# A two-block transformer kernel: gates and inverse roots of the output stages by exponential and logarithm, with the window and attention stages in another form

## The reference

```python
p = softmax(q k^T * scale + c_q - c_k, causal);  oa = (p v) * silu(za)        # forgetting attention
p = softmax([q k^T * scale in the band, sink]);  ob = (p v) * silu(zb)        # window attention
y = concat(oa, ob) @ w_out;  x = x + gate * y * rsqrt(mean(y*y) + 1e-6) * g   # first output stage
...
h = layer_norm(2**0.25 * h + concat(a * silu(ga), r * silu(gh)) @ w_out_2)    # second output stage
```

## Time and profile before

| what | value |
|---|---|
| time, median of 3 runs | 4440.61 us (4437.15 to 4445.45) |
| time of the profiled execution | 4440.12 us |
| its span, first to last instruction | 4438.6 us |
| busy: PE, DVE, ACT, POOL | 80%, 49%, 32%, 22% of the span |
| mean granted TensorE clock | 0.873 |

### The profile page before, as it was taken

How to read it: one execution, slowest core, us unless ns; L and a number is a source line. 1 busy time by engine, 2 the same in 40 slices (tenths; PEclk the granted TensorE clock), 3 DMA queues, 4 the chain that set the end, 5 groups by cost and what they waited for, 6 DMA issues and landing times. The chain is left out here.

```text
span 4438.6 us, 48060 instructions
## 1 busy us (share of the span) xinstructions
PE 3551.6 (80%) x16984; PEld 2783.3 (63%) x16984; DVE 2178.9 (49%) x4079; ACT 1440.1 (32%) x2352; POOL 996.4 (22%) x1050
## 2 busy tenths in 40 slices
PE   8299999466669999796799997935554699999978
PEld 7299988355646665675577776834444266666657
DVE  0600000322256665442489999845564345455456
ACT  0200000112124444441258873233332223333344
POOL 0120111212133320101322322343433033123010
PEclk9599999677779999898899998967777689999989
DMA  4121121200032321535212353411100454544254
GB/s 142 60 92 58 60 74 66 73 10 9 12 77 61 75 67 35 170 129 184 71 44 74 95 160 89 137 64 38 38 19 25 134 147 116 122 104 118 79 174 140
DMA packets 347338, 382.06 MB, mean 86 GB/s; under 512 B 95092, under 2 KB 276404, under 8 KB 340196
## 3 DMA queue, kind: packets, MB, share of 16 engines
q1 hardware_dynamic: 243144, 272.58, 21.6%
q10 hardware_dynamic: 98368, 77.62, 5.9%
q0 software_dynamic: 5632, 29.36, 1.7%
HBM read 260.26 MB, written 119.20 MB: 85 GB/s over the span
## 5 line engine op out<-in xcount | busy, mean ns | idle before, releaser
L447 DVE COPY p_stage<-p_bank 128x512 f32<-128x512 f32 (+4 forms) x78 | 43.3, 555 | 643.7 <-PE p_bank L409 643.7
L2429 PE MATMUL cbank<-hT_high,cw_hi 128*128 128x512 f32 x800 | 321.6, 402 | 37.9 <-POOL kpartsI L2401 16.9
L2608 DVE TENSOR_SCALAR_CACHE_REDUCE sharedI<-xI,TI 128x384 bf16<-128x384 f32 (+8 forms) x284 | 348.9, 1294 | 0.1
L2126 DVE CUSTOM_DVE_ANT_0 n_junk<-n_pM,n_chosen 128x512 bf16<-128x512 f32 (+4 forms) x352 | 200.7, 571 | 300.5 <-PE n_pM L1997 176.8
L2429 PE MATMUL cbank<-hT_high,cw_lo 128*128 128x512 f32 x800 | 315.9, 395 | 0.0
L2081 ACT ACTIVATE n_PT<-n_pS 128x512 f32<-128x512 f32 (+4 forms) x352 | 177.4, 504 | 426.6 <-PE n_pS L2035 425.1
L2429 PE MATMUL cbank<-hT_low,cw_hi 128*128 128x512 f32 x800 | 315.6, 395 | 0.0
L2052 PE MATMUL n_pO<-n_PT,n_vv 128*128 128x512 f32 (+4 forms) x704 | 315.4, 530 | 0.0
L2544 ACT ACTIVATE sharedI<-xI,biasI 128x2048 bf16<-128x2048 f32 (+2 forms) x192 | 289.8, 1511 | 48.5 <-DVE biasI L2614 48.5
L2052 PE MATMUL f_pO<-f_PT,f_vv 128*128 128x512 f32 (+3 forms) x640 | 292.6, 539 | 0.0
L2121 DVE TENSOR_REDUCE f_mxc<-f_pM 128x1 f32<-128x512 f32 (+2 forms) x320 | 190.3, 598 | 148.8 <-PE f_pM L1990 78.8
(11 more groups left out here) (432 smaller groups left out, 8755.2 us busy)
## 6 DMA issues: line engine op xcount, KB each, us to landing
n_mkt<-scratch_mask_turned ACTq DMA_DIRECT2D x256, 128.0 KB, 2.1
cw_raw<-in_w_in_dram SPq DMA_DIRECT2D x50, 512.0 KB, 4.7
wa<-in_w_ada_dram SPq DMA_DIRECT2D x16, 768.0 KB, 4.3
n_rawk<-scratch_keys SPq DMA_DIRECT2D x16, 516.0 KB, 10.0
xt<-in_x_dram POOLq DMA_DIRECT2D x16, 512.0 KB, 3.8
scratch_qk<-p_stage ACTq DMA_DIRECT2D x32, 256.0 KB, 2.4
f_rawq<-scratch_qk SPq DMA_DIRECT2D x16, 512.0 KB, 7.8
f_rawk<-scratch_qk SPq DMA_DIRECT2D x16, 512.0 KB, 9.5
```

What stands on the lines that cost most here:

```text
L447: v.tensor_copy(stage[0:rows, k, 0:width], bank[0:rows, k, 0:width]).then_inc(s_evac[k], 1)
L2126: v.tensor_tensor_reduce(junk[:, n % 2, 0:wd], pM[:, n % 2, 0:wd], chosen[:, at:at + wd], 1.0, 3.0 * NEG, ALU.add, ALU.max, accum_out=to). ...
L2429: last = pe.matmul(bank[:, p % RING, 0:wd], lhsT=w_part[pw][b][:, c, :], rhs=rhs, start=(c == 0 and a == 0), stop=(c == DC - 1 and a == 2))
L2608: own_.up(v.tensor_scalar(junk_v[:, own_.at % 2, 0:(i + 1) * P], scores(i), T[:, j:j + 1], None, compare, ALU.add, accum_out=count[:, j:j ...
```

## The change

Beside the output stages, the diff gives the window stage and the attention stages another form.

- Output stages: the gate becomes exp, log, exp on ACT, each waiting for the one before. The root becomes log and exp on ACT. DVE's mean square and reciprocal go.
- Window stage: `KZ` goes; keys are copied by one instruction, and the score product contracts over the group's own 64 partitions.
- Attention stages: `times_gate` and the folding go. DVE weighs 64 partitions x 512 columns, inverts 2 x 256 columns, multiplies by the gate from SBUF, then by the output from PSUM, which frees the output's buffer only then. Maxima are rounded and split into two columns by three further small instructions, turned by a transpose. `lead` is one less. Blanking moves from DVE to GpSimd, ahead of its constants and splits; the splits are one instruction each; the `n_` stage waits for all masks and both bias parts at its start.

The core of the diff:

```diff
@@ stage_window
-                v.tensor_copy(KZ[0:HD, par, 0, :], pT[0:HD, 0, :])
-                v.tensor_copy(KZ[HD:P, par, 1, :], pT[HD:P, 0, :]).then_inc(s_T, 1)
+                v.tensor_copy(T[:, par, 4, :], pT[:, 0, :]).then_inc(s_T, 1)
+                half = slice(HD * g, HD * g + HD)
-                        last = pe.matmul(pS[:, g, j, z, :], lhsT=T[:, par, j, :], rhs=KZ[:, kp, g, :],
+                        last = pe.matmul(pS[:, g, j, z, :], lhsT=T[half, par, j, :], rhs=T[half, kp, 4, :],
@@ stage_out, ScalarE
-                act.activation(sig[:], zg[:, b, :], ACT.Sigmoid).then_inc(s_sig, 1)
+                own_.up(act.activation(sig[:], zg[:, b, :], ACT.Exp, scale=-1.0))
+                own_.settle()
+                own_.up(act.activation(sig[:], sig[:], ACT.Ln, bias=1.0))
+                own_.settle()
+                act.activation(sig[:], sig[:], ACT.Exp, scale=-1.0).then_inc(s_sig, 1)
-                act.wait_ge(s_var, n + 1)
-                act.activation(std[:, b:b + 1], var[:, b:b + 1], ACT.Sqrt).then_inc(s_std, 1)
+                own_.settle()
+                if n >= 2:
+                    act.wait_ge(s_res[b], r)
+                own_.up(act.activation(rstd[:, b:b + 1], ssq[:, b:b + 1], ACT.Ln, bias=eps[:, 0:1], scale=1.0 / D))
+                own_.settle()
+                act.activation(rstd[:, b:b + 1], rstd[:, b:b + 1], ACT.Exp, scale=-0.5).then_inc(s_root, 1)
@@ stage_out, VectorE
-                v.wait_ge(s_ssq, n + 1)
-                v.tensor_scalar(var[:, one], ssq[:, one], 1.0 / D, 1e-6, ALU.mult, ALU.add).then_inc(s_var, 1)
-                v.wait_ge(s_std, n + 1)
-                own_.up(v.reciprocal(rstd[:, one], std[:, one]))
-                own_.settle()
+                v.wait_ge(s_root, n + 1)
@@ stage_attend
-        self.lead = self.tiles(NJ - 1) + 5
+        self.lead = self.tiles(NJ - 1) + 4
-            return sw.block_ends_with_unit(u - 3 + LEAD)
+            return sw.block_ends_with_unit(u - 2 + LEAD)
@@ stage_attend, GpSimd (start, then each head)
+            for b in range(2):
+                step(gp.memset(QA[b][HD:P, :].bitcast(F32), 0.0))
+                step(gp.memset(KA[b][HD:P, :].bitcast(F32), 0.0))
+            for b in range(2):
+                if cum2 is not None:
+                    step(gp.memset(QA[b][HD:HD + 2, :].bitcast(F32), 1.0))
+                step(gp.memset(KA[b][96:98, :].bitcast(F32), 1.0))
+            step(gp.memset(vv[:, 0, :, HD:P], 1.0))
+            step(gp.memset(vv[:, 1, :, 0:HD], 1.0))
-                for at in pieces(S):
-                    last = gp.tensor_tensor(QL[b][lower, at], rawq[lower, at], QA[b][lower, at].bitcast(F32), ALU.subtract)
-                last.then_inc(s_split, 1)
+                gp.tensor_tensor(QL[b][lower], rawq[lower], QA[b][lower].bitcast(F32), ALU.subtract).then_inc(s_split, 1)
@@ stage_attend, TensorE (values)
-                        pe.wait_ge(s_oz, B - 1)
+                        pe.wait_ge(s_norm, B - 1)
@@ stage_attend, VectorE
+                    own_.up(v.tensor_reduce(mx[:, a:b], mxc[:, B % 2, a:b, 0:n], AX.X, ALU.max))
+                own_.settle()
+                own_.up(v.tensor_scalar(mh[:], mx[:], -1.0, None, ALU.mult))
+                own_.settle()
+                own_.up(v.tensor_copy(Mx[:, :, 96], mh[:].bitcast(F32)))
+                v.scalar_tensor_tensor(Mx[:, :, 97], mx[:], -1.0, mh[:].bitcast(F32), ALU.mult, ALU.subtract
+                                       ).then_inc(s_stat, 1)
-                    last = v.tensor_reduce(Mx[:, a:b, 96], mxc[:, B % 2, a:b, 0:n], AX.X, ALU.max)
+                v.scalar_tensor_tensor(w[out], ez[den, B % 2], 1.0, pO[den, B % 2], ALU.add, ALU.mult).then_inc(s_w, 1)
-                own_.up(v.reciprocal(w[:, B % 2, z * P:(z + 1) * P], w[:, B % 2, z * P:(z + 1) * P]))
+                own_.up(v.reciprocal(rec[out, at], w[out, at]))
+                own_.up(v.tensor_tensor(tz[out], rec[out], zz[out, B % 2], ALU.mult))
-                v.tensor_tensor(G[:, B % 2], oz[:, B % 2], w[:, B % 2], ALU.mult).then_inc(s_norm, 1)
+                v.tensor_tensor(G[out, B % 2], pO[out, B % 2], tz[out], ALU.mult).then_inc(s_norm, 1)
```

More of the change, by code:

```diff
@@ L1005, in _ @@
         def _(act):
+            own_ = Tally(act, s_act)
             for k in range(DC):
@@ L1790, in stage_attend @@
         s_gp, s_dve = m.sem(n_("pool_own")), m.sem(n_("dve_own"))
[L1791 to L1792 removed]
+        s_raw, s_split = m.sem(n_("heads_loaded")), m.sem(n_("heads_split"))
         s_cum = [m.sem(n_(f"cum_loaded{b}")) for b in range(2)]
@@ L1816, in chunk_at @@
             return u + LEAD if u + LEAD < U else None
-        def two_halves():
-            return [(half, slice(z * QB4 // 2, (z + 1) * QB4 // 2)) for z, half in enumerate((lower, upper))]
         def turned_at(u):
-            return sw.block_ends_with_unit(u - 3 + LEAD)
+            return sw.block_ends_with_unit(u - 2 + LEAD)
         def chunk_width(j, r, c):
@@ L1846, in load_heads @@
                     sp.wait_ge(s_split, 6 * h)
-                for z, half in enumerate((lower, upper)):
-                    sp.dma_start(rawq[half, :], QT[h * HD:(h + 1) * HD, :]).then_inc(s_raw[z], 16)
-                    sp.dma_start(rawk[half, :], KT[h * HD:(h + 1) * HD, :]).then_inc(s_raw[z], 16)
+                for half in (lower, upper):
+                    sp.dma_start(rawq[half, :], QT[h * HD:(h + 1) * HD, :]).then_inc(s_raw, 16)
+                    sp.dma_start(rawk[half, :], KT[h * HD:(h + 1) * HD, :]).then_inc(s_raw, 16)
             def load_side(h):
@@ L1880, in store @@
                 sp.wait_ge(s_norm, B + 1)
-                for z, half in enumerate((lower, upper)):
-                    at = j * QB4 + z * QB4 // 2
-                    sp.dma_start(GT[h * HD:(h + 1) * HD, at:at + QB4 // 2], G[half, B % 2]).then_inc(s_st[B % 2], 16)
+                sp.dma_start(GT[h * HD:(h + 1) * HD, j * QB4:(j + 1) * QB4], G[halves(h)[0], B % 2]).then_inc(s_st[B % 2], 16)
             load_heads(0)
@@ L1930, in _ @@
                 step(gp.tensor_copy(mask[:], maskf[:]))
+            else:
+                step(gp.tensor_copy(ident_r[:], ident[:]))
             gp.sem_inc(s_const, 1)
@@ L1939, in split_bias @@
                 gp.wait_ge(s_bias, 2 * h + 2)
[L1941 to L1942 removed]
             for h in range(H):
                 b = h % 2
[L1946 removed]
+                gp.wait_ge(s_raw, 64 * h + 64)
                 if h >= 2:
                     gp.wait_ge(s_sc, UH * (h - 1))
[L1949 to L1954 removed]
+                gp.tensor_copy(QA[b][lower], rawq[lower]).then_inc(s_split, 1)
+                gp.tensor_copy(KA[b][lower], rawk[lower]).then_inc(s_split, 1)
                 gp.wait_ge(s_split, 6 * h + 2)
@@ L2005, in turn_max @@
                 for r in range(4):
-                    last = pe.matmul(pR[:, r], lhsT=Mx[:, r], rhs=ident_r[:], start=True, stop=True)
+                    last = pe.transpose(pR[:, r], Mx[:, r], ident[:])
                 last.then_inc(s_tr, 1)
@@ L2142, in weight, with invert @@
                 v.wait_ge(s_ez, B + 1)
-                for half, at in two_halves():
-                    last = v.scalar_tensor_tensor(w[half, B % 2], ez[den, B % 2, at], 1.0, pO[den, B % 2, at],
-                                                  ALU.add, ALU.mult)
-                last.then_inc(s_w, 1)
-            def times_gate(B):
+                v.scalar_tensor_tensor(w[out], ez[den, B % 2], 1.0, pO[den, B % 2], ALU.add, ALU.mult).then_inc(s_w, 1)
+            def invert(B, z):
+                out = halves(B // NJ)[0]
+                at = slice(z * 2 * P, (z + 1) * 2 * P)
+                v.wait_ge(s_w, B + 1)
+                own_.up(v.reciprocal(rec[out, at], w[out, at]))
@@ L2149, in times_gate, with finish @@
+            def finish(B):
                 out = halves(B // NJ)[0]
                 v.wait_ge(s_z[B % 2], 32 * (B // 2) + 32)
-                for half, at in two_halves():
-                    last = v.tensor_tensor(oz[half, B % 2], pO[out, B % 2, at], zz[out, B % 2, at], ALU.mult)
-                last.then_inc(s_oz, 1)
-            def invert(B, z):
-                v.wait_ge(s_w, B + 1)
-                own_.up(v.reciprocal(w[:, B % 2, z * P:(z + 1) * P], w[:, B % 2, z * P:(z + 1) * P]))
```

102 lines of the change are left out of this document (34 added, 68 removed).

## The result

| kernel | median | range |
|---|---|---|
| before | 4442.53 us | 4437.15 to 4445.45 (4 runs) |
| after | 4677.04 us | 4673.80 to 4683.14 (4 runs) |

A forecast was written before the change was run, and what follows sets the result against it. PE bounds attention and `o1_`, a PE/DVE/ACT wait chain the window stage, a DVE/ACT loop `o2_`. Window +38, `f_` +64, `o1_` +5, `n_` +28, `o2_` +27: together +162, 4602 us, range 4518 to 4665.

The forecast's parts named there:

- Window stage: Window stage: score products over 64 partitions lower the granted clock, +43, less one key copy, -4.7; net +38 us.
- the bound that 32-partition products gave: Window stage: products over few partitions don't raise the clock, so of bounds 0 and +43 us it took +43.
- rival 1: Window stage: the clock stays, so the stage gives -5 in place of +38; total 4559 us, chance 18 in 100.
- The copy's 4.7 us: Window stage: one of two key copies goes, 0.29 us x 16 on the path from keys to scores, -4.7 us.
- Output stages: `o1_` and `o2_`: each alternation of log and exp loads a table; +4.7 and +27.5 us, `o2_` tile 13.04 us.
- Rival 3: Output stages: logarithm and exponential share a table, -4 in place of +32; total 4566 us, chance 7 in 100.
- Attention, start: Start of `f_` and `n_`: GpSimd's blanking delays the first product, +8; later start and mask waits, +6 us.
- The terms of 3.7 and 2.0 us a block: `f_` block ends: DVE's longer work 3.7 us, seven times; gate product waiting for GpSimd 2.0 us, six times.
- rival 5: Attention block ends at upper bounds: gate product waits 4.9 us, output's buffer freed late; 4673 us, chance 11 in 100.
- And +0.7 at each block's maxima: Attention block ends: DVE's work for the maxima grows by only 0.7 us a block.
- the product with the gate now reads two SBUF operands: Attention block ends: this DVE product waits for GpSimd's 4.9 us instruction, 2.0 us in six `f_` heads, 1.5 in `n_`.
- Rival 2: Attention stages: PE's slack hides the block ends, `f_` 8 + 10 + 1.7; total 4538 us, chance 12 in 100.

The follow-up runs named there:

- the run with half products: Kernel before, with window-stage score products contracting over the group's own 64 partitions, both key copies and zeros kept: 4483.50 us, +43.4, ratio 1.0096.

## Why the forecast was right in its direction and wrong in its size

- **Window stage**, forecast +38, alone +37: right, and the clock fell as forecast. Taking the end of the bound that 32-partition products gave was right too; rival 1 falls by the run with half products. That the sum fits so well is in part luck. The score and value products took 19 and 24 us more, in sum as priced. The transposes of the probabilities between them (line 829) took 24 us more too, 62.9 in place of 39.4, and were not in the sum, while PE's wait for ScalarE's copies fell by 26. The copy's 4.7 us was not resolved. The Trainium skill (TensorE: Matmul & The Clock Gate, Part 1) says that the clock follows how busy TensorE has been. Here PE was busy 339 of 455 us against 266 of 425, in part because the slower products last longer, and the clock was lower.
- **Output stages**, forecast +32, alone +30: right, `o2_` by 29 and `o1_` by 4. The tile is 13.04 us, as worked out. Rival 3 falls: four loads a tile. The Trainium skill (ScalarE: Activation LUTs, Table sets) says that a logarithm and the exponential behind it need one load. The trace disagrees: 32 loads of 1283 ns on each of four lines.
- **Attention, start**, forecast +14, alone +16.5: right in sum. In `f_` the first product came 6.6 us later, 7.4 forecast. In `n_` the wait for masks behind the first product was 8.4 us, more than thought, but it did not show in the stage's own time.
- **Attention, block ends, longer work.** The terms of 3.7 and 2.0 us a block gave 42 us in `f_` for block ends and maxima together, 44 with the tail. With short splits the changed kernel lost 58 there, 7 of them at the start: 51. The sum is short by about what the late buffer costs alone, 7.6, which it had at nothing (only rival 5 names it). In `n_` the changed kernel with short splits lost 35, where 19 were forecast; the block ends alone are 14 of them, and what the rest is stays open.
- **The step that failed is "And +0.7 at each block's maxima".** The mechanism of the hold was in the forecast, but for one instruction only: "the product with the gate now reads two SBUF operands", 2.0 us in six heads of `f_` and 1.5 in six of `n_`, 21 us. That product was held for 15.3 us in `f_` and 0.3 in `n_`. The maxima's small multiplication, copy and last instruction were priced as instructions of 4 columns that wait for nobody. They were held until GpSimd's long instruction was over, 17 us in `f_` and 53 in `n_`. The long splits as a whole cost 66 us (60 by the two stages' own times), where 21 were forecast: that is some 40 to 45 of the 75 us missed.
- The trace of before had the price, in a stage that the change does not touch. There VectorE multiplies 14 columns by a constant, 32 times, 175 ns as a rule. One of these met a GpSimd subtraction and ended with it:

```profile
2596.15 2.25 DVE L2614 TENSOR_SCALAR biasI<-TI 128x14 f32<-128x14 f32 x1
```

```profile
2595.95 2.41 POOL L2382 TENSOR_TENSOR cw_lo<-cw_raw,cw_hi 128x1024 fp32r<-128x1024 f32 x1
```

- The earlier trace rows showed a product of two SBUF operands held; what else on VectorE can be held was not asked. The Trainium skill (SBUF — State Buffer, SBUF: two separate sides) says that VectorE and GpSimd share one port pair that either holds for a whole instruction, VectorE in instructions with two SBUF inputs or in a mode that uses both ports. The Trainium skill (VectorE: DVE Perf Modes, The perf-mode tier table) gives copies and tensor-scalar operations in float32 such a mode. The runs agree: held were the copy, the multiplication by a constant and instructions of two SBUF operands; reductions and, in the example above, the inverse were not.
- **Rival 2** falls: the block ends alone cost 56 us, and PE's slack did not hide them. **Rival 5** gave the nearest time, 4673, and that is luck: it has the product and the late buffer, and not the maxima.

Open: why long splits cost 115 us with the maxima alone but 66 in the whole change. Held time moves from one instruction to the next, and the block ends may move the steps at which they meet GpSimd; no run separates that. Open too are some 16 us that `n_` lost beyond its forecast and beyond the long splits.

## What to carry to other kernels

Before a GpSimd instruction is made longer, list every VectorE instruction that can meet it, the smallest ones first: a hold lasts as long as what is left of GpSimd's instruction, however small the one that is held. If a duration in the trace doesn't fit the columns, look at what GpSimd ended at that moment, and sum "busy less count times shortest" as held time. Search the whole trace for it, the untouched stages too. Put the blanking that only a later head needs behind the first head's work, on an engine that is idle there (5 us of the start of `f_` here).

## What the runs showed of the hardware

- A VectorE copy of 4 columns took 0.17 us, and 4.47 beside a GpSimd subtraction of 4.49; in the same kernels no reduction into 4 columns took over 0.18.
- The granted clock of the window stage fell from 0.71 to 0.50 when its score products contracted over 64 in place of 128 partitions, at +43 us.
- Each change between logarithm and exponential on ScalarE loaded a table, 1283 ns, 32 times on each of four lines.
- Freeing the output's buffer later cost 5.6 us of PE's waits alone and 21.6 with VectorE's longer work, in `f_`: an edit that is cheap alone can cost more beside another.
